# QKV projections of two attention kinds as three rounded passes, with their weights split beside the attention itself

## The reference

```python
for i in range(DEPTH):                                  # 4
    h = h + 0.5 * swiglu(rms_norm(h, norm_ffn1[i]), ffn1_w_gate_up[i], ffn1_w_down[i])
    hn = rms_norm(h, norm_mix[i])
    ...                                                 # sb, moba, mla, sb
    h = h + mix
    h = h + 0.5 * swiglu(rms_norm(h, norm_ffn2[i]), ffn2_w_gate_up[i], ffn2_w_down[i])
```

## Time and profile before

| what | value |
|---|---|
| median of 3 runs (lowest, highest) | 3988.57 us (3985.23, 3990.15) |
| time of the profiled execution | 3986.17 us |
| its span | 3984.4 us |
| mean granted TensorE clock | 0.975 |
| PE busy | 3782.0 us (95%) |
| DVE busy | 2155.3 us (54%) |
| ACT busy | 1505.7 us (38%) |
| POOL busy | 1114.0 us (28%) |

### The profile page before, as it was taken

How to read it: one execution, slowest core, us unless ns; L and a number is a source line. 1 busy time by engine, 2 the same in 40 slices (tenths; PEclk the granted TensorE clock), 3 DMA queues, 4 the chain that set the end, 5 groups by cost and what they waited for, 6 DMA issues and landing times.

```text
span 3984.4 us, 46609 instructions
## 1 busy us (share of the span) xinstructions
PE 3782.0 (95%) x17679; PEld 2989.3 (75%) x17679; DVE 2155.3 (54%) x2221; ACT 1505.7 (38%) x1883; POOL 1114.0 (28%) x574
## 2 busy tenths in 40 slices
PE   8999999999999899999999898998999998998999
PEld 6866888767888678887578786687778786686787
DVE  5644766426666356664466545346555545337554
ACT  4344444334433343443443332233434332234343
POOL 6700848304656018482056001030000001031000
PEclk9999999999999999999999999998999999999999
DMA  8634767446766157674376453301455553201463
GB/s 264 228 105 154 244 210 250 151 127 212 253 205 224 44 176 255 201 252 127 111 239 205 158 167 101 109 33 53 169 190 180 169 169 101 97 32 68 164 202 127
DMA packets 493256, 649.69 MB, mean 163 GB/s; under 512 B 16075, under 2 KB 393442, under 8 KB 493090
## 3 DMA queue, kind: packets, MB, share of 16 engines
q1 hardware_dynamic: 472356, 569.62, 44.3%
q0 software_dynamic: 19584, 75.50, 5.4%
q10 hardware_dynamic: 1150, 2.29, 0.2%
HBM read 646.29 MB, written 1.05 MB: 162 GB/s over the span
## 4 chain that ended last, share of the span: by engine, by line
issue 59%; POOLq 19%; PE 13%; POOL 7%; ACT 1%; SPq 1%; DMA 0%; DVE 0%; DVEq 0%; ACTq 0%
POOLq L602 7%; POOLq L604 6%; POOLq L606 5%; PE bank L1287 3%; PE bank L932 3%; POOL mod_zone L609 2%; POOL modrow L609 2%; PE bank L904 1%; PE bank L1423 1%; PE bank L1434 1%; POOL modrow L591 1%; POOL mod_zone L591 1%; PE bank L911 1%; PE bank L913 1%; PE bank L912 1%
## 5 line engine op out<-in xcount | busy, mean ns | idle before, releaser
L2144 DVE TENSOR_TENSOR wproj_lo<-wproj,wproj_hi 128x2048 fp32r<-128x2048 f32 x252 | 748.1, 3005 | 132.4 <-ACT wproj_hi L1671 132.4
L932 PE MATMUL bank<-wproj_hi,x_hi 128*128 128x512 f32 x2112 | 540.7, 398 | 21.6 <-DVE arena L2235 11.9
L932 PE MATMUL bank<-wproj_lo,x_hi 128*128 128x512 f32 x2112 | 534.4, 396 | 0.0
L932 PE MATMUL bank<-wproj_hi,x_lo 128*128 128x512 f32 x2112 | 524.8, 391 | 0.0
L932 PEld LDWEIGHTS bank<-wproj_hi,x_hi 128*128 128x128 f32 x2112 | 397.3, 190 | 116.1 <-issue 28.7
L566 POOL TENSOR_SCALAR rstd<-sumsq 128x1 f32<-128x1 f32 x38 | 9.1, 239 | 1698.6 <-ACT tok L1654 1698.6
L1711 ACT CAST actT_hi<-bank 128x512 fp32r<-128x512 f32 x132 | 77.4, 587 | 1071.8 <-PE bank L959 1071.8
L1671 ACT CAST wproj_hi<-wproj 128x2048 fp32r<-128x2048 f32 x252 | 469.8, 1910 | 14.1 <-DMA wproj<-in_ffn_w_gate_up 14.1
L932 PEld LDWEIGHTS bank<-wproj_hi,x_lo 128*128 128x128 f32 x2112 | 399.4, 189 | 84.2
L932 PEld LDWEIGHTS bank<-wproj_lo,x_hi 128*128 128x128 f32 x2112 | 387.6, 188 | 76.6
L904 PE MATMUL bank<-wproj,xT 128*128 128x384 f32 (+2 forms) x1216 | 421.2, 502 | 8.2 <-issue 4.7
(11 more groups left out here) (425 smaller groups left out, 5152.0 us busy)
## 6 DMA issues: line engine op xcount, KB each, us to landing
wproj<-in_ffn_w_gate_up SPq DMA_DIRECT2D x336, 512.0 KB, 6.0
wdown<-in_ffn_w_down SPq DMA_DIRECT2D x132, 1024.0 KB, 5.0
wproj<-in_ffn_w_gate SPq DMA_DIRECT2D x84, 512.0 KB, 5.0
wproj<-in_ffn_w_up SPq DMA_DIRECT2D x84, 512.0 KB, 6.6
wproj<-in_w_in SPq DMA_DIRECT2D x40, 1024.0 KB, 7.3
mod_zone<-in_mod_w POOLq DMA_DIRECT2D x36, 1024.0 KB, 6.1
modrow<-in_mod_w POOLq DMA_DIRECT2D x36, 1024.0 KB, 5.8
wproj<-in_sb_w_qkv SPq DMA_DIRECT2D x48, 512.0 KB, 5.4
```

The costliest lines, as they stand in the source:

```text
L932: last = nc.tensor.matmul(proj_ps[t][:, :], rounded(x_part[of_x](c)[:, toks]), rounded(w_part[of_w][:, c, :]), start=start and c == 0, sto ...
L2144: V.tensor_tensor(rounded(wproj_lo[w.odd][:, cols]), src[:, cols], wproj_hi[w.odd][:, cols], ALU.subtract).then_inc(cols_lo, 1)
```

## The change

The QKV projection of sb and moba becomes three passes of rounded products with 384 columns, as the FFN has them: high x high, low tokens x high weights, high tokens x low weights. So a token tile takes 24 products in place of 8.

* ScalarE rounds each pair's weights in two halves of 128x1536 (`round_pair`). Pair 0 is rounded in the last FFN step between the silu instructions, pair 1 after the squares at the entry, pair k+2 in pair k around the first `evac`.
* VectorE makes the low parts in two halves (`rest_of_pair`). Pair 0: after the last FFN step's own low parts. In sb, pair k+1 in pair k: one half behind the logits, one behind the outputs, both ahead of the scan. In moba, pair 1 ahead of the loop and pair k+2 in pair k, between logits and rotation.
* The tokens are split at the entry: `round_x` on ScalarE (ahead of each square) into the unused last 1024 columns of the two `wproj_hi` buffers, and `x_lo` on VectorE.
* SyncE loads a pair in six transfers of 256 KB, half by half. Pair 0 is issued ahead of the last FFN rows.

```diff
+            def heads_in_halves(w_qkv, i, w):
+
+                room(w)
...
+                for half in range(2):
+                    chunks = slice(half * BC, (half + 1) * BC)
+                    for s in range(3):
+                        sp.dma_start(dst[:, chunks, s], src[:, chunks, s, bass.ds(i.n(P), P)]
+                                     ).then_inc(pair_in[w.odd][half], DMA)
...
                 if after is not None:
                     columns(Step(0), Step(n.load + FF_STEPS), Step(n.ffn + FF_STEPS), *after)
+                if pairs is not None:
+                    heads_in_halves(pairs, Step(0), Step(n.load + FF_STEPS))
                 rows(Step(FF_STEPS - 1), Step(n.ffn + FF_STEPS - 1))
...
+                def project_in_halves(i, w, t, mid):
...
+                    if k == 0:
+                        pe.wait_ge(x_rounded, 4 * n.entries + 2 * (t + 1))
+                    for c in range(KC):
+                        if t == 0 and c % BC == 0:
+                            pe.wait_ge(pair_hi, 2 * (n.split + k) + 1 + c // BC)
+                        if mid is not None and c == BC:
+                            mid()
+                        nc.tensor.matmul(proj_ps[t][:, 0:384], rounded(pair_x_hi(c)[:, toks]), rounded(hi[:, c, :]),
+                                         start=(c == 0), stop=False, skip_group_check=True)
+                    if k == 0:
+                        x_here(t)
+                    for c in range(KC):
+                        nc.tensor.matmul(proj_ps[t][:, 0:384], rounded(x_lo[:, c, toks]), rounded(hi[:, c, :]),
+                                         start=False, stop=False, skip_group_check=True)
+                    for c in range(KC):
+                        if t == 0 and c % BC == 0:
+                            pe.wait_ge(pair_lo, 2 * (n.split + k) + 1 + c // BC)
+                        last = nc.tensor.matmul(proj_ps[t][:, 0:384], rounded(pair_x_hi(c)[:, toks]),
+                                                rounded(lo[:, c, :]), start=False, stop=(c == KC - 1),
+                                                skip_group_check=True)
+                    last.then_inc(proj_done, 1)
...
                     if kind == "sb":
                         softplus_tails(i, u)
+                        if ahead_pair:
+                            round_pair(split_pair, w.plus(2), [0])
                         if more:
                             evac(i.plus(1), w.plus(1), 0)
                         if k:
                             copy_outputs(i.plus(-1), c.plus(-1))
+                        if ahead_pair:
+                            round_pair(split_pair, w.plus(2), [1])
                         exp_arg(i, u, 0)
...
-            def squares():
+            def squares(parts=None):
 
                 for t in range(NT):
+                    if parts is not None:
+                        round_x(t, parts)
                     square(t)
...
-                squares()
+                squares(pair_x_hi_parts if l % 3 != 2 else None)
+                if l % 3 != 2:
+                    round_pair(Step(n.split + 1), Step(n.load + 1))
...
+            def rest_of_pair(i, w, parts=range(2)):
+
+                for half in parts:
+                    cols = pair_half(half)
+                    v.wait_ge(pair_hi, i.n(2, 1 + half))
+                    V.tensor_tensor(rounded(wproj_lo[w.odd][:, cols]), wproj[w.odd][:, cols], wproj_hi[w.odd][:, cols],
+                                    ALU.subtract).then_inc(pair_lo, 1)
...
+                    if k + 1 == FF_STEPS and pairs_next:
+                        rest_of_pair(Step(n.split), w.plus(1))
...
                     if kind == "sb":
+                        if k + 1 < pairs:
+                            rest_of_later(i, 1, [0])
                         if k > 0:
                             outputs(i.plus(-1), c.plus(-1))
+                        if k + 1 < pairs:
+                            rest_of_later(i, 1, [1])
                         stick(i, u, 0)
...
                     else:
+                        if kind == "moba" and k + 2 < pairs:
+                            rest_of_later(i, 2)
                         if k + ahead < pairs:
                             prepare(i.plus(ahead))
```

101 lines of the change are left out of this document (75 added, 26 removed).

## The result

| | before | after |
|---|---|---|
| median (lowest, highest) | 3986.9 us (3982.7, 3990.15), 4 runs | 3955.48 us (3951.5, 3957.75), 4 runs |
| time of the profiled execution | 3986.17 us | 3951.5 us |
| its span, mean granted clock | 3984.4 us, 0.975 | 3949.8 us, 0.974 |

The ratio is 0.9922, with an interval of 0.9906 to 0.9937: 0.8% faster, 31 us. In the profiled executions the difference is 34.7 us. The prediction was 3943 us, with a range of 3930 to 3963. The measured median lies inside the range, but outside the forecast proper of 3936 to 3952.

The account below looks back on a forecast made before the run. TensorE was taken as the bound, with room on VectorE and ScalarE. Gains of 26.2 + 1.6 + 3.6 + 12.9 = 44.3 us off 3986.2 gave 3941.9; the median lies 2.4 above, and 3943 was predicted, range 3930 to 3963.

Parts of the forecast that it names:

- the forecast proper: Whole kernel: the prediction's own case without its rivals, 3936 to 3952 us, chance 0.60.
- the sum: Whole kernel: gains of 26.2 + 1.6 + 3.6 + 12.9 = 44.3 us from sb, entry and moba, giving 3941.9.
- the low parts that are late in each pair: Rival, sb and moba: 0.7 us lost in each of 21 pairs, gain 29.6, time 3957; chance 0.22.
- TensorE's part: Projection of a token tile: 24 products at 0.172 us, 4.13 in place of 5.22, saving 1.09; 52.3 us over 48 tiles.
- The higher of the two readings of rows 3: Projection: a 384-column product costs the FFN's 512-column 0.2268 us less 128 cycles at 2.4 GHz (0.0533), so 0.1735.
- the rival that a narrower product is no cheaper: Projection: 384 columns cost as much as 512, a tile takes 5.44 us, time 3998; chance 0.04.
- Pairs 2 to 7 of sb: sb attention, two layers: the low parts cost no wait, 2.18 us gained for each of 6 pairs, 26.2 us.
- with 0.05 us to spare: sb pairs 2 to 7: low-part half 1 ends at 248.31, TensorE's 21st product needs it at 248.36.
- Pair 1 of sb: First round of sb: TensorE waits 1.4 us for the low parts, 0.8 of 2.18 left, 1.6 us in two layers.
- The entry: Entry, pair 0: TensorE waits from 215.7 to 216.5 for VectorE's update; gain 1.2 us, 3.6 in three layers.
- the charge of 0.3 us a pair for the rotation: moba pairs 1 to 7: rotation stands behind the low parts, so 1.88 us gained a pair, 12.9 us in all.
- Transfers and the end of the FFN: Pair loads and last FFN step: cost nothing; VectorE at most 0.73 us late against a cover of 1.24.

Follow-up runs that it names:

- the second, 3946.01: The changed kernel run again with nothing edited, against the kernel before: 3946.01 us, ratio 0.9900 (0.9884 to 0.9917).
- the two-pass kernel: Changed kernel without the pass of high tokens with low weights, whose low parts are still made and waited for: 3930.65 us, ratio 0.9857 against the kernel before.
- the half behind the scan: Changed kernel with the second half of sb's low part moved behind the scan of head 0: 4023.4 us, ratio 1.0096 against the kernel before.
- the second pair: Second profiles of both kernels, nothing edited: before 3981.92 us in a single execution; changed 3946.01 us, ratio 0.9900, its profiled execution 3957.69 us.
- the one square: Changed kernel with one more 128x1024 square by ScalarE ahead of the second stack's last mixer: 3946.11 us, ratio 0.9907 against the kernel before.

## Why the prediction was right

The parts were right: at an undisturbed clock the attentions gave what the sum says, to 3 us. That the time fell into the range is in part luck. The range reached up to 3963 for the low parts that are late in each pair, which didn't come; the forecast without the rivals was 3936 to 3952. The first measurement, 3955.48, lies outside it, the second, 3946.01, inside. The difference is a term that the prediction didn't have, the clock.

**TensorE's part was right, and 0.12 us a tile too large.** Foretold was 0.172 us a product and 1.09 gained a tile. It was 0.1734, and the first group of a tile takes 0.1 us longer than the others, so the gain was 5.22 - 4.25 = 0.97. The higher of the two readings of rows 3, 128 cycles of 2.4 GHz less than 0.2268, gives 0.1735 and was exact. The rule of the Trainium skill that the prediction weighed (TensorE: Matmul & The Clock Gate, Back-to-back issue gap), which gives 162.5 ns at 384 columns, isn't borne out: 173.4 ns here, and 110 at 192 columns. The section gives it for a product by itself, not for a stream of products with their loads. Nor did the rival that a narrower product is no cheaper come true.

**Pairs 2 to 7 of sb.** 2.18 was foretold for each, 1.96 came: 23.5 in place of 26.2 us, all of it the tile's size. "Just in time, with 0.05 us to spare" was too tight: the margin is 0.3. The prediction added whole records, but on VectorE the next instruction starts up to 0.1 us ahead of the end of the record before it: 240.56 to 245.43 is 4.87 us for logits, two halves and outputs, where the sum said 5.13. So the rival with low parts that are late in each pair fell. That its mechanism is real is shown by the two-pass kernel, where the wait appears once TensorE is earlier, and by the half behind the scan.

**Pair 1 of sb.** Foretold were 1.4 us of wait and 0.8 of gain; the timeline has 0.2 for half 0 and 1.0 for half 1, and the time from this projection to the next fell from 15.49 to 14.80: 0.7 of gain.

**The entry.** The foretold wait of 0.8 us ahead of the turn is there, 0.78 us, released by the hidden rows. The second copy out of PSUM came at 224.44 against 226.39, with a layer that had begun 0.95 earlier: 1.0 gained in place of 1.2.

**moba.** Here the step that failed is the charge of 0.3 us a pair for the rotation. The rotation waits for ScalarE's copy of the second tile (784.15 + 0.58), which comes just behind the low part, so nothing is charged: 15.25 - 13.31 = 1.94 a pair, 13.6 us in place of 12.9. The worry had its ground: where TensorE is earlier still, in two passes, it waits 1.04 us for the rotation.

**Transfers and the end of the FFN** cost nothing, as foretold. The early place of pair 0's transfers is part of that (with them behind the rows, ScalarE and then TensorE wait). The subtractions of pair 0 ended so that VectorE took the hidden rows at 207.98, 2.43 ahead of TensorE's turn, where it had been 2.53.

**The sum.** By these sizes it is 23.5 + 1.4 + 3.0 + 13.6 = 41.5 us against the foretold 44.3. The stretches at a clock of 1.00 give the same 41.5, and those of the pair of profiles it was made for 42.0. (The foretold 3941.9 and the 2.4 that the median lies above it make 3944.3; 3943 was put down. That changes nothing.) The missing 7.3 us up to the 34.7 of the whole lie outside: 9.5 lost in the last mixer, 5.2 gained in the first mixer of the second stack, 3.0 lost in all the rest. The prediction looked at the granted clock in the stretches that it changed, and took 1.00 and 0.99 for it. In the first profile of the changed kernel the three attentions have 1.00, 0.99 and 0.98, each the clock that the same attention had before:

```profile
210.41:354.90 144.49, 133.18 (x746) 110.44 (x744) 90.64 (x118) 88.48 (x137) 1.49 (x4) 1.00 0.36 110
742.52:882.25 139.73, 132.99 (x746) 111.83 (x745) 71.49 (x126) 67.70 (x137) 1.49 (x4) 0.99 0.37 113
1806.48:1954.24 147.76, 136.46 (x746) 112.07 (x744) 90.66 (x118) 88.42 (x137) 1.49 (x4) 0.98 0.35 107
```

In the second pair the clocks differ, and 35.4 us are left of the 41.5. What the prediction didn't have is a term for the clock, there and above all elsewhere: work that is moved in time can meet a lower level in a stretch that it doesn't touch. That a shift is enough is shown for the last mixer by the one square. Why a shift does it, what it is that the clock follows there, stays open. So does why all kernels with the changed attention but not moved further had the long mixer in their profiles, though it starts more than 1200 us behind the last changed attention. For the timed executions, which have no such table, only their mean clock speaks (0.973 with 3957.69 us, 0.977 with 3942.25 in one kernel).

## What to carry to other kernels

Price a narrower product by taking the saved columns at the clock's rate off a wider one of the same kind in the same trace, and look for a floor, as the 0.11 us here, before you go narrower. When work is moved onto the side engines, what counts is at which product it is needed: the same subtraction cost nothing ahead of the scan and 34 to 35 us a layer behind it. Before a gain or loss of a few tenths of a per cent is put down to an edit, compare the untouched stretches of both traces: here one of them differed by 9.5 us, and a delay of 1.13 us took that away in the profile. And compare changed stretches at the same granted clock: that turned 42.0 and 35.4 us into one 41.5.

## What the runs showed of the hardware that I had not expected

A rounded product with its own load takes 0.2268 us at 512 columns, 0.1734 at 384 and 0.110 at 192: the first step down is the 128 columns at 2.4 GHz (0.0534), the second less than its 192 columns (0.063 where they would be 0.080). A wait of TensorE of 3.26 us was followed by products at half the rate, 1.4 us more on the same pair; the next one, of 3.25 us, was not. In a long run of small products the granted clock stayed at 1.2 GHz for 37.5 us or came back to 2.4 GHz after 10.2, and a shift of 1.13 us in when the mixer begins decided it, worth 9.3 us. In eight profiles that long piece began at the same place of the work to 0.2 us.
